# The second layer's scores, routing and experts in one phase, with the first tile routed in four parts

## The chip, the cores and the metric

One NeuronCore of a Trainium2 chip runs the whole program. The metric is the device time of one execution in microseconds. The engines are TensorE (PE), VectorE (DVE), ScalarE (ACT), GpSimd (POOL) and SyncE (SP), each with an instruction queue of its own; they meet only at semaphores. SP starts plain transfers, GpSimd starts the gathers.

## The reference

Two blocks of two layers each, for 256 tokens of width 1024. The part at hand is the feed-forward sublayer of the first block, run for its second layer (`l = 1`), where only x is updated:

```python
def peer_ffn(h, w_query, sub_keys, u_tab, v_tab):          # chunks of 128 tokens
    q = (hc @ w_query).reshape(128, 8, 2, 64)
    s = einsum('chpd,hpnd->chpn', q, sub_keys)              # 8 heads, 2 lists of 128 scores
    s_top, i_top = top_k(s, 16)
    cand = s_top[:, :, 0, :, None] + s_top[:, :, 1, None, :]   # 16 x 16 sums a head
    best, pos = top_k(cand, 16)
    eid = take_along_axis(i_top0 * 128 + i_top1, pos)       # 16 experts a head, 128 a token
    gate = softmax(best)
    act = gelu(einsum('chkd,cd->chk', u_tab[eid], hc)) * gate
    return einsum('chk,chkd->cd', act, v_tab[eid])
```

Each token needs 128 rows of `u_tab` and 128 rows of `v_tab`, each of 4 KB.

## The kernel before, in words

The program is a row of phases. `phase` opens a block with one program per engine and ends with a barrier of all engines. A function given as `ahead` is run by SP in a phase to load what the next phase reads first. `done` makes an engine wait for its own instruction's semaphore. Buffers are SBUF tiles; `ps` is PSUM, 8 banks of 512 columns.

For the second layer three phases follow each other:

1. `norm_modulate` computes h from x; ahead it loads the first half of `w_query` into `wring` slot 0 (`first_unit`).
2. `scores` (lines 1317 to 1402). SP loads the keys, the numbers 0 to 15 (`iot`) and the second half of `w_query`. For each of 8 heads TensorE computes the query (L1361), ScalarE copies it (L1387), TensorE multiplies it with the keys (L1352), and ScalarE copies the scores of tile 0 (128 tokens) to `sc` (L1374) and those of tile 1 to `stage` (L1379), from where SP stores them to DRAM (`kept`). VectorE follows head by head: `route_list` ranks each of a head's two lists (`best16`, L1242 to L1246), `route_sums` makes the 256 sums (L1257, L1259), `route_head` ranks them. After the eighth head `route_tail` runs for all heads at once: `route_shift` (L1268), `route_pick` (L1276 to L1286, six instructions over 128 x 16 = 2048 columns, which turn positions into list entries), `route_ids` (L1290, L1291, the expert numbers `eid`), `route_gate` (L1297 to L1299) after ScalarE's Exp (L1314).
3. `experts` (from line 1943). The work is 2 tiles x 16 groups `G` of `GRP = 8` expert columns; a head is two groups. For each group GpSimd issues 8 gathers of u rows into `gu` (L2036) and 8 of v rows into `gv` (L2045), 512 KB each. There is one buffer per column: a gather of `gu` waits for the dot product of the group before on the same buffer, a gather of `gv` for the accumulation (`summed`, columns 0 to 3) or the matmul (`mixed`, columns 4 to 7) of the group before. VectorE runs, in this order for each group, `dot` (8 dot products with the token rows `htok`, L2116), `route_next`, `weigh` (L2123, after ScalarE's Gelu, L2065) and `add_up` (4 accumulations, L2134 and L2136). ScalarE makes diagonal matrices (L2074) and TensorE adds the other four columns with them (L2010). At the start TensorE turns h (`turn_h`, L1984) and ScalarE copies it to `htok` (`copy_h`, L2053).

`route_next` routes tile 1 beside the groups of tile 0, out of `sc`, which SP has loaded back from DRAM (L2084): 3 lists in each of the first groups until 16 are done, the sums at G = 5, one head in each of G = 6 to 13, and the tail at G = 14. Beside tile 1 the phase builds rows of a bias table for the next block.

The order of work on each engine is the order in which the code is written. GpSimd enters the `experts` phase only after the barrier that ends `scores`.

Of the kernel before, what the change touches and what calls it, by code (L numbers as in the profile page):

```python
# [97 lines left out]
class Program:  # L98
# [1134 lines left out]
    def memory_scores(self):  # L1233
        self.sc = self.sb("sc", [P, 16, NKEY])
        self.qp = self.sb("qp", [P, 2, 2 * S])
        self.keys = self.sb("keys", [P, H1, 2 * NKEY])
        self.stage = self.sb("stage", [P, 2, 3, 2 * NKEY])

# [9 lines left out]
    def route_list(self, dve, sig, g):  # L1248

        self.best16(dve, sig, self.sc[:, g, :], self.sc[:, g, :], self.top[:, g, :], self.topi[:, g, :])  # L1250
# [15 lines left out]
    def route_shift(self, dve, shifted, t):  # L1266
        g3 = self.gate[:, t, :].rearrange("p (h k) -> p h k", h=H1)
        done(dve, self.nc.vector.tensor_tensor(g3, self.best[:], self.best[:, :, 0:1].to_broadcast([P, H1, TOPK]), ALU.subtract),  # L1268
             shifted)

    def route_pick(self, dve, sig, part):

        v = self.nc.vector
        bpos, bhi, bhf, hot = self.bpos, self.bhi, self.bhf, self.hot
        if part == 0:
            done(dve, v.tensor_scalar(bhi[:, 0, :], bpos[:], 4, None, ALU.logical_shift_right), sig)  # L1276
            done(dve, v.tensor_scalar(bhi[:, 1, :], bpos[:], 15, None, ALU.bitwise_and), sig)
            done(dve, v.tensor_copy(bhf[:], bhi[:]), sig)
            return
        c = part - 1  # L1280
        tf = self.topf[:].rearrange("p (h c) k -> p h c k", c=2)
        done(dve, v.tensor_tensor(hot, bhf[:, c, :].unsqueeze(2).to_broadcast([P, COLS, TOPK]),
                                  self.iot[:].unsqueeze(1).to_broadcast([P, COLS, TOPK]), ALU.is_equal), sig)
        hh = hot.rearrange("p (h k) i -> p h k i", h=H1)
        done(dve, v.tensor_tensor(hh, hh, tf[:, :, c, :].unsqueeze(2).to_broadcast([P, H1, TOPK, TOPK]), ALU.mult), sig)
        done(dve, v.tensor_reduce(self.esel[:, c, :], hot, AX, ALU.add), sig)  # L1286

    def route_ids(self, dve, sig, l, t):
        v, esel = self.nc.vector, self.esel
        done(dve, v.scalar_tensor_tensor(esel[:, 0, :], esel[:, 0, :], float(NKEY), esel[:, 1, :], ALU.mult, ALU.add), sig)  # L1290
        done(dve, v.tensor_scalar(self.eid[:, t, :], esel[:, 0, :], float(l * NEXP), None, ALU.add), sig)  # L1291

    def route_gate(self, dve, sig, exped, t, nth):
        v, gsum = self.nc.vector, self.gsum
        g3 = self.gate[:, t, :].rearrange("p (h k) -> p h k", h=H1)
        dve.wait_ge(exped.sem, nth)
        done(dve, v.tensor_reduce(gsum[:], g3, AX, ALU.add), sig)  # L1297
        done(dve, v.reciprocal(gsum[:], gsum[:]), sig)
        done(dve, v.tensor_tensor(g3, g3, gsum[:].unsqueeze(2).to_broadcast([P, H1, TOPK]), ALU.mult), sig)  # L1299

    def route_tail(self, dve, sig, shifted, exped, l, t, nth=1):
        self.route_shift(dve, shifted, t)
        for part in range(3):
            self.route_pick(dve, sig, part)
        self.route_ids(dve, sig, l, t)
        self.route_gate(dve, sig, exped, t, nth)

    def route_exp(self, act, shifted, exped, t):
        act.wait_ge(shifted.sem, 1)
        self.route_exp_now(act, exped, t)  # L1310

    def route_exp_now(self, act, exped, t):
        g = self.gate[:, t, :]
        self.nc.scalar.activation(g, g, ACT.Exp).then_inc(exped.sem, 1)  # L1314

    def scores(self, l, T, weights):


        nc, ps, a, hT = self.nc, self.ps, self.a, self.hT
        tiles = T // P  # L1320
        qp, keys, sc, stage = self.qp, self.keys, self.sc, self.stage

        def slot(s):
            return self.wring[:, s, 0:KD * 512].rearrange("p (k n) -> p k n", k=KD)

        def bank(h, t):
            return ps[:, 4 + 2 * (h % 2) + t // 2, (t % 2) * 256:(t % 2) * 256 + 256]
        with self.phase("loaded", "w1", "full", "copied", "sfull", "first", "rest", "shifted", "dve_done", "exped",
                        "stored0", "stored1") as (
                block, loaded, w1, full, copied, sfull, first, rest, shifted, dd, exped, st0, st1):  # L1330
            st = (st0, st1)

            @block.sync
            def _(sp):
                sp.dma_start(keys[:], a["keys"][l]).then_inc(loaded.sem, 16)
                sp.dma_start(self.iot[:], a["iota16"]).then_inc(loaded.sem, 16)
                sp.dma_start(slot(1), weights(1)).then_inc(w1.sem, 16)
                for h in range(H1):
                    sp.wait_ge(rest.sem, h + 1)
                    sp.dma_start(self.kept[1:tiles, :, h * 256:(h + 1) * 256].rearrange("t p n -> p t n"),  # L1340
                                 stage[:, h % 2, 0:tiles - 1, :]).then_inc(st[h % 2].sem, 16)
                for s in range(2):
                    sp.wait_ge(st[s].sem, 16 * H1 // 2)

            @block.tensor
            def _(pe):
                def score(h):
                    pe.wait_ge(copied.sem, h + 1)
                    if h >= 2:
                        pe.wait_ge(rest.sem, h - 1)  # L1350
                    for t in range(tiles):
                        m = nc.tensor.matmul(bank(h, t), qp[:, h % 2, t * P:(t + 1) * P], keys[:, h, :], start=True, stop=True)  # L1352
                    m.then_inc(sfull.sem, 1)

                for h in range(H1):
                    if h == 4:
                        pe.wait_ge(w1.sem, 16)
                    if h >= 4:
                        pe.wait_ge(copied.sem, h - 3)
                    for k in range(KD):  # L1360
                        m = nc.tensor.matmul(ps[:, h % 4, 0:T], slot(h // 4)[:, k, (h % 4) * P:(h % 4 + 1) * P],  # L1361
                                             hT[:, k, 0:T], start=k == 0, stop=k == KD - 1)
                    m.then_inc(full.sem, 1)
                    if h == 0:
                        pe.wait_ge(loaded.sem, 32)
                    else:
                        score(h - 1)
                score(H1 - 1)

            @block.scalar  # L1370
            def _(act):
                def out(h):
                    act.wait_ge(sfull.sem, h + 1)
                    nc.scalar.activation(sc[:, 2 * h:2 * h + 2, :].rearrange("p a n -> p (a n)"), bank(h, 0),  # L1374
                                         ACT.Copy).then_inc(first.sem, 1)
                    if h >= 2:
                        act.wait_ge(st[h % 2].sem, 16 * (h // 2))
                    for t in range(1, tiles):
                        ins = nc.scalar.activation(stage[:, h % 2, t - 1, :], bank(h, t), ACT.Copy)  # L1379
                        if t == tiles - 1:  # L1380
                            ins.then_inc(rest.sem, 1)

                for h in range(H1):
                    act.wait_ge(full.sem, h + 1)
                    if h >= 2:
                        act.wait_ge(sfull.sem, h - 1)
                    nc.scalar.activation(qp[:, h % 2, 0:T], ps[:, h % 4, 0:T], ACT.Copy).then_inc(copied.sem, 1)  # L1387
                    if h >= 1:
                        out(h - 1)
                out(H1 - 1)  # L1390
                self.route_exp(act, shifted, exped, 0)

            @block.vector
            def _(dve):
                dve.wait_ge(loaded.sem, 32)
                for h in range(H1):
                    dve.wait_ge(first.sem, h + 1)
                    for g in (2 * h, 2 * h + 1):
                        self.route_list(dve, dd, g)
                    self.route_sums(dve, dd, slice(h, h + 1))  # L1400
                    self.route_head(dve, dd, h)
                self.route_tail(dve, dd, shifted, exped, l, 0)
# [538 lines left out]
    def experts(self, l, tiles, tables):  # L1941
# [25 lines left out]
        with self.phase("turned", "hready", "dotted", "gelud", "weighed", "summed", "diagd", "mixed", "joined", "turned2",  # L1967
# [114 lines left out]
            def _(sp):  # L2082
# [19 lines left out]
                if tables:  # L2102
                    for k in range(4):
                        sp.wait_ge(stored[k].sem, 64)
# [739 lines left out]
```

## Time and profile before

| | us |
|---|---|
| median of 3 runs (lowest, highest) | 4629.44 (4618.14, 4631.32) |
| the profiled execution, its own time | 4630.75 |
| its span in the trace | 4629.0 |
| PE, DVE, POOL, ACT busy in the span | 3687.6, 2507.9, 1346.4, 632.5 |
| scores phase, first matmul to last VectorE instruction | 2366.85 to 2449.04 |
| first gather; last instruction of `experts` | 2450.70; 3169.3 |

A row of a timeline gives start, duration, engine, line, operation, output and inputs, count, and in brackets the idle time before it with what ended it. A row of the stage table gives the busy time of each engine in a stretch with its number of instructions, the granted TensorE clock as a share of full speed, the share of time in which the DMA engines were busy, and what they moved.

### The profile page before, as it was taken

The page shows a single profiled execution, that of the slowest core. Times are in us where ns is not written, and L with a number is a line of the kernel's source. Part 1 is how long each engine was busy: PE and PEld are TensorE (multiplying, and loading weights), DVE is VectorE, ACT ScalarE, POOL GpSimd, SP SyncE. Part 2 cuts the span into 40 slices and gives each one's busy share as a digit, 9 for nine tenths or more (in the row PEclk, how much of TensorE's full clock was granted, in tenths as well). Part 3 has the DMA queues.
Part 4 walks back from the last instruction along what each step waited for, and adds up shares of the span by engine and source line. Part 5 has one row for each costly group of instructions (what it writes and reads, how often), then busy time and mean ns, then how long its engine had stood idle before and what let it go on. Part 6 is the DMA issues. An engine that isn't in the chain of part 4 may idle for free. (4 is left out here: it accounts for less than half of the span.)

```text
span 4629.0 us, 46599 instructions
## 1 busy us (share of the span) xinstructions
PE 3687.6 (80%) x15786; PEld 2896.0 (63%) x15786; DVE 2507.9 (54%) x4821; ACT 632.5 (14%) x1702; POOL 1346.4 (29%) x1156
## 2 busy tenths in 40 slices
PE   5889897588998999957962444546999898999898
PEld 2467685577777877734851111214886787887787
DVE  2365476977788677744558888673534101433300
ACT  2231111310000000023110001101012201011200
POOL 0260000146566566604006777771000000000000
PEclk7879998899999999977986677777996899997799
DMA  4308454689999999910928999996850343861243
GB/s 140 128 31 242 132 162 163 203 308 409 409 408 374 409 409 407 403 62 26 255 77 309 375 384 377 411 403 248 297 175 28 123 150 130 275 215 46 91 154 100
DMA packets 564560, 1093.55 MB, mean 236 GB/s; under 512 B 29796, under 2 KB 344164, under 8 KB 563590
## 3 DMA queue, kind: packets, MB, share of 16 engines
q1 hardware_dynamic: 412776, 549.92, 35.2%
q0 software_dynamic: 147456, 536.94, 29.7%
q10 hardware_dynamic: 4128, 4.19, 0.3%
q8 instruction: 105, 1.72, 0.2%
q14 instruction: 95, 0.78, 0.1%
HBM read 1074.16 MB, written 16.78 MB: 236 GB/s over the span
## 5 line engine op out<-in xcount | busy, mean ns | idle before, releaser
L2010 PE MATMUL ps<-gv,diag 128*128 128x512 f32 x512 | 302.0, 756 | 392.7 <-DMA gv<-in_v_tab,eid 290.0
L1728 POOL DMA_INDIRECT gu<-in_u_tab,eid x256 | 351.4, 1373 | 859.1 <-DVE gate L1299 509.1
L2457 PE MATMUL ps<-hT,wring 128*128 128x256 f32 x2560 | 559.2, 379 | 0.2 <-DMA wring<-in_ffn_w_up 0.2
L1693 PE MATMUL ps<-hT,wring 128*128 128x256 f32 x2048 | 481.0, 389 | 75.9 <-DVE hT L1866 75.9
L2457 PEld LDWEIGHTS ps<-hT,wring 128*128 128x128 f32 x2560 | 486.3, 190 | 66.7 <-issue 0.6
L1693 PEld LDWEIGHTS ps<-hT,wring 128*128 128x128 f32 x2048 | 387.1, 193 | 163.9 <-DVE hT L1866 113.2
L2010 PEld LDWEIGHTS ps<-gv,diag 128*128 128x128 f32 x512 | 123.0, 248 | 570.0 <-issue 425.4
L1684 PE MATMUL ps<-hT,wring 128*128 128x256 f32 x2048 | 466.4, 381 | 6.8 <-DMA wring<-in_u_first 6.8
L1684 PEld LDWEIGHTS ps<-hT,wring 128*128 128x128 f32 x2048 | 391.6, 191 | 60.7 <-DMA wring<-in_u_first 6.9
L1890 DVE SCALAR_TENSOR_TENSOR wring<-gv,wgt,wring 128x1024 f32<-128x1024 f32 x254 | 326.5, 1286 | 115.6 <-DMA gv<-in_v_tab,eid 111.9
L2116 DVE CUSTOM_DVE_ANT_0 junk<-gu,htok 128x1024 f32<-128x1024 f32 x256 | 313.7, 1225 | 130.5 <-DMA gu<-in_u_tab,eid 121.8
L2036 POOL DMA_INDIRECT gu<-in_u_tab,eid x256 | 275.8, 1077 | 349.7 <-POOLq L134 272.0
L1873 DVE CUSTOM_DVE_ANT_0 gu<-gu,htok 128x1024 f32<-128x1024 f32 x256 | 313.2, 1223 | 116.9 <-DMA gu<-in_u_tab,eid 114.4
L1735 POOL DMA_INDIRECT gv<-in_v_tab,eid x256 | 293.0, 1145 | 141.0 <-issue 73.3
L2468 PE MATMUL ps<-hff,wring 128*128 128x256 f32 x1408 | 310.4, 379 | 0.0
L2524 DVE TENSOR_TENSOR hff<-sgf,ps 128x256 f32<-128x256 f32 x88 | 35.6, 419 | 502.2 <-ACT sgf L2497 502.2
L2045 POOL DMA_INDIRECT gv<-in_v_tab,eid x256 | 269.1, 1051 | 79.2 <-issue 76.2
L2468 PEld LDWEIGHTS ps<-hff,wring 128*128 128x128 f32 x1408 | 267.5, 190 | 36.4
L1000 PE MATMUL ps<-hT,wring 128*128 128x256 f32 x768 | 179.7, 388 | 13.5 <-SPq L134 8.0
L1000 PEld LDWEIGHTS ps<-hT,wring 128*128 128x128 f32 x768 | 148.1, 195 | 35.4 <-issue 15.0
L2136 DVE SCALAR_TENSOR_TENSOR acc<-gv,wgt,acc 128x1024 f32<-128x1024 f32 x126 | 162.0, 1285 | 10.1 <-DMA gv<-in_v_tab,eid 5.9
L2497 ACT ACTIVATE sgf<-ps 128x256 f32<-128x256 f32 x88 | 33.7, 383 | 818.7 <-PE ps L2457 771.0
(332 smaller groups left out, 4836.9 us busy)
## 6 DMA issues: line engine op xcount, KB each, us to landing
wring<-in_u_first SPq DMA_DIRECT2D x128, 512.0 KB, 9.0
wring<-in_v_tab SPq DMA_DIRECT2D x128, 512.0 KB, 6.8
lslot<-in_ada_w SPq DMA_DIRECT2D x32, 1536.0 KB, 10.9
wring<-in_ffn_w_gate SPq DMA_DIRECT2D x44, 1024.0 KB, 7.5
wring<-in_ffn_w_up SPq DMA_DIRECT2D x44, 1024.0 KB, 10.0
wring<-in_ffn_w_down SPq DMA_DIRECT2D x44, 1024.0 KB, 5.0
wring<-in_w_in SPq DMA_DIRECT2D x72, 512.0 KB, 6.7
wring<-in_w_mod SPq DMA_DIRECT2D x28, 1024.0 KB, 7.0
```

Of the source, the lines that this page charges most:

```text
L1000: nc.tensor.matmul(ps[:, b, 0:T], slot(s, b)[:, k, :], hT[:, k, at:at + T], start=k == 0, stop=k == KD - 1)
L1684: m = nc.tensor.matmul(ps[:, 4 + e % 2, 0:S], uslot[:, e % 3, k, :], hT[:, k, S:2 * S], start=k == 0, stop=k == KD - 1)
L1693: m = nc.tensor.matmul(ps[:, n // 2, (n % 2) * S:(n % 2 + 1) * S], vslot[:, e % 2, n * P:(n + 1) * P], act_[:, e % 3, :], start=e == 0 and ...
L1728: nc.gpsimd.indirect_dma_start(gu[:, n % RING, :], None, ub, bass.IndirectOffsetOnAxis(ap=eid[:, n // COLS, n % COLS:n % COLS + 1], axis=0 ...
L1735: nc.gpsimd.indirect_dma_start(gv[:, n % RING, :], None, vb, bass.IndirectOffsetOnAxis(ap=eid[:, n // COLS, n % COLS:n % COLS + 1], axis=0 ...
L1873: v.tensor_tensor_reduce(out=gu[:, j, :], in0=gu[:, j, :], in1=htok[:, n // COLS, :], scale=1.0, scalar=0.0, op0=ALU.mult, op1=ALU.add, ac ...
L1890: ins = v.scalar_tensor_tensor(acc, gv[:, j, :], wgt[:, s, j:j + 1], acc, ALU.mult, ALU.add)
L2010: m = nc.tensor.matmul(ps[:, mixed_banks(t) + b, :], diag[:, s, i, :], gv[:, BYDVE + i, b * 512:(b + 1) * 512], start=first, stop=last)
L2036: nc.gpsimd.indirect_dma_start(gu[:, j, :], None, ub, bass.IndirectOffsetOnAxis(ap=eid[:, t, n * GRP + j:n * GRP + j + 1], axis=0)).then_i ...
L2116: v.tensor_tensor_reduce(out=junk[:], in0=gu[:, j, :], in1=htok[:, t % 2, :], scale=1.0, scalar=0.0, op0=ALU.mult, op1=ALU.add, accum_out= ...
L2457: m = nc.tensor.matmul(ps[:, 4 + 2 * s + n, q * S:(q + 1) * S], up_slot(s, q)[:, k, n * P:(n + 1) * P], hT[:, k, 0:S], start=k == 0, stop= ...
L2468: m = nc.tensor.matmul(ps[:, n // 2, (n % 2) * S:(n % 2 + 1) * S], down_slot(s)[:, k, n * P:(n + 1) * P], hff[:, s, k, :], start=first and ...
```

## The change

The `scores` phase is gone and its work goes to the start of `experts`. The keys are loaded in the norm phase before, into the half of `xT` that held the context (`query_and_keys`). The scores of tile 1 are copied to the free half of `hT` (`later`) and never leave the chip. The first tile is routed in four parts (`PARTS`): head 0, head 1, heads 2 and 3, heads 4 to 7; the tail functions take a range of heads. GpSimd waits on `listed` only where a group needs the numbers of a new part (`PART_OF_GROUP`). VectorE ranks head 0, chooses its numbers, does the same with head 1, then starts the groups; the other heads of tile 0 are ranked in groups 0 to 5, their numbers chosen in groups 1 and 6, and tile 1 is routed in groups 7 to 14. The turn of h stands behind the query of the third head on TensorE, its copy behind that of the fourth on ScalarE.

```diff
+    def query_and_keys(self, l, weights):
+        def start(sp, landed):
+            sp.dma_start(self.wring[:, 0, 0:KD * 512].rearrange("p (k n) -> p k n", k=KD), weights(0)).then_inc(landed.sem, 16)
+            sp.dma_start(self.xT[:, :, S:2 * S], self.a["keys"][l]).then_inc(landed.sem, 16)
+            sp.dma_start(self.iot[:], self.a["iota16"]).then_inc(landed.sem, 16)
+            return 3
+        return start
...
-        LISTS, HEADS, TAIL = 3, 6, 14
+        PARTS = [(0, slice(0, 1)), (0, slice(1, 2)), (0, slice(2, 4)), (0, slice(4, 8)), (1, slice(0, 8))]
+        PART_OF_GROUP = {0: 1, 2: 2, 4: 3, 8: 4, 16: 5}
+        TAIL_AT = {2: 1, 3: 6, 4: 14}
+        LIST_FROM, HEADS_FROM = 7, 11
+        qp, keys, sc, later = self.qp, self.xT[:, :, S:2 * S], self.sc, self.hT[:, :, S:2 * S]
...
             def _(pe):
-                turn_h(0)
+                for h in range(H1):
...
+                    m.then_inc(full.sem, 1)
+                    if h:
+                        score(h - 1)
+                    if h == 2:
+                        turn_h(0)
+                score(H1 - 1)
...
             def _(pool):
-                    if n == 0 and t >= 1:
-                        pool.wait_ge(routed.sem, ROUTED * (t - 1) + EID)
+                    if G in PART_OF_GROUP:
+                        pool.wait_ge(listed.sem, PART_OF_GROUP[G])
...
             def _(act):
-                copy_h(0)
+                for h in range(H1):
...
+                    nc.scalar.activation(qp[:, h % 2, :], ps[:, h % 4, 0:S], ACT.Copy).then_inc(copied.sem, 1)
+                    if h >= 1:
+                        out(h - 1)
+                    if h == 3:
+                        copy_h(0)
+                out(H1 - 1)
+                exp_part(0)
+                exp_part(1)
...
             def _(dve):
+                def head_lists(h):
+                    dve.wait_ge(first.sem, h + 1)
+                    for g in (2 * h, 2 * h + 1):
+                        self.route_list(dve, routed, g)
+                    self.route_sums(dve, routed, slice(h, h + 1))
+                    self.route_head(dve, routed, h)
+
+                def pick_part(i):
+                    t, heads = PARTS[i]
+                    self.route_shift(dve, shifted, t, heads)
+                    for part in range(3):
+                        self.route_pick(dve, routed, part, heads)
+                    self.route_ids(dve, routed, l, t, heads, listed)
...
+                def route_ahead(G):
+                    if G < 2:
+                        head_lists(2 + G)
+                    elif G < 6:
+                        head_lists(2 + G)
+                    elif LIST_FROM <= G < LIST_FROM + 4:
...
+                        for g in range(4 * (G - LIST_FROM), 4 * (G - LIST_FROM) + 4):
+                            self.route_list(dve, routed, g, later[:, g // 2, g % 2 * NKEY:(g % 2 + 1) * NKEY])
+                    elif HEADS_FROM <= G < HEADS_FROM + 3:
+                        if G == HEADS_FROM:
+                            self.route_sums(dve, routed, slice(0, H1))
+                        for h in range(3 * (G - HEADS_FROM), min(3 * (G - HEADS_FROM) + 3, H1)):
+                            self.route_head(dve, routed, h)
+                    for i, at in TAIL_AT.items():
+                        if at == G:
+                            pick_part(i)
+                            gate_part(i)
+
+                for h in range(2):
+                    head_lists(h)
+                    pick_part(h)
                 for G in range(ALL):
...
-                    route_next(G)
+                    if G == 0:
+                        gate_part(0)
+                        gate_part(1)
+                    route_ahead(G)
                     weigh(G)
                     add_up(G)
...
-            self.norm_modulate(S, A_G2, 3, 4, ahead=self.first_unit(w_of("w_query")))
-            self.memory_scores()
-            self.scores(l, S, w_of("w_query"))
-            self.release(mixer)
+            self.norm_modulate(S, A_G2, 3, 4, ahead=self.query_and_keys(l, w_of("w_query")))
             self.memory_gather()
-            self.experts(l, 2, True)
+            self.experts(l, w_of("w_query"))
```

How the instructions stand now is shown at two places of VectorE's queue. The first is the end of routing of tile 0 and the first dot product. Before, behind the ranking of the eighth head (`ISA junk` is a dot product):

```order
L1246 MAX_INDEX bpos<-best,wring 128x8
L1268 TENSOR_TENSOR gate<-best 128x128
...
L1282 TENSOR_TENSOR wring<-bhf,iot 128x2048
L1285 TENSOR_TENSOR wring<-wring,topf 128x2048
L1286 TENSOR_REDUCE esel<-wring 128x128
...
L1291 TENSOR_SCALAR eid<-esel 128x128
L1297 TENSOR_REDUCE gsum<-gate 128x8
L1298 RECIPROCAL gsum<-gsum 128x8
L1299 TENSOR_TENSOR gate<-gate,gsum 128x128
L126 UNCONDITIONAL_BRANCH
L2106 UNCONDITIONAL_BRANCH
L2116 ISA junk,dots<-gu,htok 128x1024
```

Now, behind the ranking of head 1 (that of head 0 ends in the same rows):

```order
L1240 MAX_INDEX bpos<-best,wring 128x8
L1266 TENSOR_TENSOR gate<-best 128x16
...
L1281 TENSOR_TENSOR wring<-bhf,iot 128x256
L1284 TENSOR_TENSOR wring<-wring,topf 128x256
L1285 TENSOR_REDUCE esel<-wring 128x16
...
L1290 SCALAR_TENSOR_TENSOR esel<-esel 128x16
L1291 TENSOR_SCALAR eid<-esel 128x16
L2073 ISA junk,dots<-gu,htok 128x1024
```

The dot products begin behind two heads instead of eight, the wide instructions have 256 columns, and no end of a phase lies between. The second place is group 1, behind its dot products, where before three lists of tile 1 stood and then `L2123 TENSOR_TENSOR wgt<-wgt,gate 128x8`:

```order
L1253 TENSOR_TENSOR wring<-top 128x256
...
L1240 MAX_INDEX bpos<-best,wring 128x8
L1266 TENSOR_TENSOR gate<-best 128x32
...
L1284 TENSOR_TENSOR wring<-wring,topf 128x512
L1285 TENSOR_REDUCE esel<-wring 128x32
L1290 SCALAR_TENSOR_TENSOR esel<-esel 128x32
L1291 TENSOR_SCALAR eid<-esel 128x32
L1298 TENSOR_REDUCE gsum<-gate 128x2
L1299 RECIPROCAL gsum<-gsum 128x2
L1300 TENSOR_TENSOR gate<-gate,gsum 128x32
L2080 TENSOR_TENSOR wgt<-wgt,gate 128x8
L2093 SCALAR_TENSOR_TENSOR acc<-gv,wgt,acc 128x1024 x4
```

Head 3 of tile 0 and the numbers of heads 2 and 3 stand between the dot products of group 1 and its accumulations.

## Rows read from the trace of the kernel before

**Rows 1.** Stage table: scoring, gathers of tile 0 (columns: section above)

```profile
2372.00:2404.00 32.00, 31.74 (x148) 27.59 (x146) 24.22 (x102) 7.90 (x23) 0.00 (x0) 1.00 0.23 82
2451.00:2778.00 327.00, 133.27 (x237) 55.17 (x235) 270.04 (x505) 24.35 (x76) 254.74 (x238) 0.68 0.99 379
```

**Rows 2.** Timeline: routing of tile 0 on DVE, first gather, first dot product

```profile
2377.51 0.29 DVE L1242 MAX8 top<-sc 128x8 f32<-128x128 f32 x1 [12.26 <-ACT sc L1374]
...
2384.38 0.30 DVE L1242 MAX8 top<-sc 128x8 f32<-128x128 f32 x1
...
2432.48 0.29 DVE L1268 TENSOR_TENSOR gate<-best 128x128 f32<-128x128 f32 x1
...
2447.93 0.23 DVE L1291 TENSOR_SCALAR eid<-esel 128x128 uint32<-128x128 f32 x1
...
2450.70 1.02 POOL L2036 DMA_INDIRECT gu<-in_u_tab,eid  x1 [272.00 <-POOLq L134]
...
2456.67 1.23 DVE L2116 CUSTOM_DVE_ANT_0 junk<-gu,htok 128x1024 f32<-128x1024 f32 x1 [7.63 <-DMA gu<-in_u_tab,eid]
```

**Rows 3.** Timeline of DVE in the experts phase: groups 0, 13, 14 and 15

```profile
2473.48 0.17 DVE L2123 TENSOR_TENSOR wgt<-wgt,gate 128x8 f32<-128x8 f32 x1
...
2755.98 0.43 DVE L1242 MAX8 best<-wring 128x8 f32<-128x256 f32 x1
...
2758.49 0.17 DVE L2123 TENSOR_TENSOR wgt<-wgt,gate 128x8 f32<-128x8 f32 x1
...
2777.79 0.29 DVE L1268 TENSOR_TENSOR gate<-best 128x128 f32<-128x128 f32 x1
...
2794.46 0.17 DVE L2123 TENSOR_TENSOR wgt<-wgt,gate 128x8 f32<-128x8 f32 x1
...
2799.94 1.22 DVE L2116 CUSTOM_DVE_ANT_0 junk<-gu,htok 128x1024 f32<-128x1024 f32 x1
...
2815.87 1.22 DVE L2116 CUSTOM_DVE_ANT_0 junk<-gu,htok 128x1024 f32<-128x1024 f32 x1
```

**Rows 4.** Timeline of ACT: the Gelu of groups 0, 6, 18 and 31

```profile
2467.95 0.21 ACT L2065 ACTIVATE wgt<-dots 128x8 f32<-128x8 f32 x1 [13.54 <-DVE dots L2116]
...
2602.22 0.21 ACT L2065 ACTIVATE wgt<-dots 128x8 f32<-128x8 f32 x1 [16.82 <-DVE dots L2116]
...
2869.63 0.21 ACT L2065 ACTIVATE wgt<-dots 128x8 f32<-128x8 f32 x1 [5.78 <-DVE dots L2116]
...
3148.64 0.21 ACT L2065 ACTIVATE wgt<-dots 128x8 f32<-128x8 f32 x1 [18.63 <-DVE dots L2116]
```

**Rows 5.** Idle of DVE before tile 0's dot products (us, times); POOL at group 15

```profile
  DMA gu<-in_u_tab,eid: 48.4, 38
...
2796.75 1.32 POOL L2045 DMA_INDIRECT gv<-in_v_tab,eid  x1 [1.52 <-DVE acc L2136]
```

**Rows 6.** Entry: issue and landing of w_query, end of the norm, last score copy

```profile
2354.51 0.37 SPq L146 DMA_DIRECT2D wring<-in_w_query  x1
...
wring<-in_w_query SPq DMA_DIRECT2D x1, 2048.0 KB, 8.5
...
2362.07 4.04 ACT L342 ACTIVATE hT<-hT,mod,aff 128x256 f32<-128x256 f32 x8 [2.35 <-DVE hT L364]
...
2404.06 0.38 ACT L1379 ACTIVATE stage<-ps 128x256 f32<-128x256 f32 x1
```

**Rows 7.** Timeline: gathers beside wide DVE instructions and a dot product

```profile
2507.84 1.22 DVE L2116 CUSTOM_DVE_ANT_0 junk<-gu,htok 128x1024 f32<-128x1024 f32 x1
2508.91 0.97 POOL L2045 DMA_INDIRECT gv<-in_v_tab,eid  x1 [0.30 <-issue]
...
2781.29 2.29 DVE L1285 TENSOR_TENSOR wring<-wring,topf 128x2048 f32<-128x2048 f32 x1
2782.37 2.02 POOL L2036 DMA_INDIRECT gu<-in_u_tab,eid  x1 [0.30 <-issue]
2784.70 0.94 POOL L2036 DMA_INDIRECT gu<-in_u_tab,eid  x1 [0.31 <-issue]
```

More of the change, by code:

```diff
@@ L1264, in route_head, with gates_of @@
         self.best16(dve, sig, self.cand[:, h, :], self.cand[:, h, :], self.best[:, h, :], self.bpos[:, h * TOPK:(h + 1) * TOPK])
[L1266 to L1271, printed above, removed]
+    def gates_of(self, t, heads):
+        return self.gate[:, t, heads.start * TOPK:heads.stop * TOPK]
@@ L1279, in route_pick @@
             return
         c = part - 1
[L1281 to L1286, printed above, removed]
@@ L1301, in route_tail @@
[L1301 to L1313, printed above, removed]
-        self.nc.scalar.activation(g, g, ACT.Exp).then_inc(exped.sem, 1)
@@ L1316, in scores @@
[L1316 to L1402, printed above, removed]
@@ new lines, in route_ids, with route_gate @@
+    def route_ids(self, dve, sig, l, t, heads=slice(0, H1), ready=None):
+        v, at = self.nc.vector, slice(heads.start * TOPK, heads.stop * TOPK)
+        e0, e1 = self.esel[:, 0, at], self.esel[:, 1, at]
+        done(dve, v.scalar_tensor_tensor(e0, e0, float(NKEY), e1, ALU.mult, ALU.add), sig)
+        done(dve, v.tensor_scalar(self.eid[:, t, at], e0, float(l * NEXP), None, ALU.add), ready or sig)
+    def route_gate(self, dve, sig, exped, t, nth, heads=slice(0, H1)):
+        v, gsum = self.nc.vector, self.gsum[:, heads]
+        n = heads.stop - heads.start
+        g3 = self.gates_of(t, heads).rearrange("p (h k) -> p h k", h=n)
+        dve.wait_ge(exped.sem, nth)
+        done(dve, v.tensor_reduce(gsum, g3, AX, ALU.add), sig)
+        done(dve, v.reciprocal(gsum, gsum), sig)
+        done(dve, v.tensor_tensor(g3, g3, gsum.unsqueeze(2).to_broadcast([P, n, TOPK]), ALU.mult), sig)
@@ L1404, in memory_scores_first, with route_exp_now @@
+    def route_exp_now(self, act, exped, t, heads=slice(0, H1)):
+        g = self.gates_of(t, heads)
+        self.nc.scalar.activation(g, g, ACT.Exp).then_inc(exped.sem, 1)
     def memory_scores_first(self):
@@ L1998, in row, with score @@
                                      stop=True).then_inc(rowfull.sem, 1)
-                turn_h(0)
+                def score(h):
+                    pe.wait_ge(copied.sem, h + 1)
+                    if h >= 2:
+                        pe.wait_ge(rest.sem, h - 1)
+                    for t in range(2):
+                        m = nc.tensor.matmul(ps[:, 4 + h % 2, t * 256:(t + 1) * 256], qp[:, h % 2, t * P:(t + 1) * P], keys[:, h, :],
+                                             start=True, stop=True)
+                    m.then_inc(sfull.sem, 1)
+                for h in range(H1):
+                    if h == 4:
+                        pe.wait_ge(w1.sem, 16)
+                    if h >= 4:
+                        pe.wait_ge(copied.sem, h - 3)
+                    for k in range(KD):
+                        m = nc.tensor.matmul(ps[:, h % 4, 0:S], slot(h // 4)[:, k, (h % 4) * P:(h % 4 + 1) * P],
+                                             hT[:, k, 0:S], start=k == 0, stop=k == KD - 1)
+                    m.then_inc(full.sem, 1)
[4 more added lines that the diff above has]
+                score(H1 - 1)
                 for G in range(ALL):
```

108 lines of the change are left out of this document (53 added, 55 removed).

## Prediction

> **What bounds the kernel now.** I read the page first. Then the stage table, the timelines of VectorE, ScalarE and GpSimd around the change, and the waits. In the stage that the change touches the DMA engines are busy for 0.99 of the time and GpSimd issues one gather behind another, while TensorE has only 133 of 327 us to do [rows 1]. In the 32 us before that the order is the reverse: DMA share 0.23, TensorE at full clock, and VectorE routing the first tile [rows 1]. That is the stretch to look at. Its first head is picked from 2377.51 to 2384.38, that is 6.87 us a head (16 lists of 128, the pair sums, one list of 256), the eighth ends at 2432.48, the choice of the expert numbers for all heads lasts to 2448.16, and the first gather starts at 2450.70, the first dot product at 2456.67 [rows 2]. For 73 us almost nothing moves on the memory side, and afterwards the memory side is the bound.
>
> How much of a gather period VectorE needs decides what an early start is worth. A group of 8 expert columns is 16 gathers, 8 dot products and 4 accumulations. From the dot product at 2799.94 to that at 2815.87, with no wait for data, it is 15.93 us; where routing stands between, it hides ScalarE's Gelu (0.3 us), so I use **15.65 us a group** [rows 3]. Gelu starts give the period: 2467.95 to 2602.22 is 6 groups of 22.38 us, 2602.22 to 2777.79 is 8 of 21.95, and tile 1 runs at 21.46 (2869.63 to 3148.64, 13 groups) [rows 3, 4]. In the first six groups VectorE also ranks 3 lists of the next tile (5.53 us, 2467.95 to 2473.48), in the next eight one head (2.51 us, 2755.98 to 2758.49) [rows 3, 4]. So the load is 21.2, 18.2 and 15.65 us and VectorE waits 1.2, 3.8 and 5.8 us a group. In all it waits 48.4 us for the gathered u rows in tile 0, 7.6 of them before the first dot [rows 2, 5].
>
> **The change, part by part.**
>
> *Start of the gathers.* Scores come out as before. Head 0 is ranked at 2384.35, then its numbers are chosen alone: six wide instructions on 256 elements instead of 2048. A 256-wide one takes 0.43 and a 2048-wide one 2.29 us [rows 3, 7], a line of 0.16 + 0.00104 a column. Six at 0.46 with the gap and six narrow ones at 0.2 make 4.0 us, so the numbers are there at 2388.35 and the first gather follows some 0.3 us later, 62 us earlier than before. Head 1 costs 6.87 + 4.0 and VectorE reaches the first dot product at 2399.2; the first row landed 6.0 us after its issue before [rows 2], at 2394.7 now, so it does not wait. **The first dot product moves by -57.5 us.** The copy of the scores of tile 1 stays on the chip: 2 MB of stores and loads go, among them the 1 MB load beside the first gathers; I count nothing, since the stores lie under routing and the load under a wait of VectorE that now is gone.
>
> *What VectorE then does beside the gathers.* Before, the 15 groups from the first dot to that at 2799.94 held 15 x 15.65 - 0.5 (the first accumulation is a short one) = 234.2 us, 16 lists 29.5, pair sums 2.7, eight heads 20.1 and the tail 16.7 (2777.79 to 2794.46) [rows 3]: 303.2 us of work in 343.3 us, 40.1 us waited. Now the same 234.2 plus, by group: G0 the gates of heads 0 and 1 and head 2, 8.1; G1 head 3, the numbers for heads 2 and 3 (six at 0.72, narrow 1.2) and gates, 13.0; G2 to G5 one head each, 27.5; G6 the numbers for heads 4 to 7 (six at 1.25, narrow 1.4) and gates, 9.6; G7 to G10 four lists each, 29.5; G11 pair sums and three heads, 10.2; G12 7.5; G13 5.0; G14 the tail, 16.7. Sum 127.1, in all **361.3 us**. Nearly every group is now at 22.5 us or more, above the gathers' own pace, so VectorE is the bound of tile 0 and GpSimd waits.
>
> *Waits that stay.* They shrink with load: 5.8, 3.8, 1.2 us at 15.65, 18.2, 21.2. Bounds for a group at 22.5 to 23.2: nothing (after the 32 us tail group the next two run without a wait [rows 3]), and 1.2. I take 0.5, 1.2 for G13 alone and nearly nothing for G0, G1, G6, G11 and G14: 6 us in all, between 0 and 18.
>
> *Sum to the dot product of G15.* -57.5 + (361.3 + 6.0 - 343.3 = 24.0) = **-33.5 us**. At that point GpSimd stands as before: it is held at the gather of v behind the tail, since that buffer is freed by the accumulation (2796.75) [rows 5]. From there tile 1 is the same work, bound by the gathers, so the lead stays as it is.
>
> *Entry.* Keys and the 16 numbers now load during the norm, behind the query weights. The weights landed 8.5 us after 2354.51; the norm ends with ScalarE at 2366.11 [rows 6]. One more MB at the 379 GB/s of [rows 1] is 2.8 us: 2365.8, hidden by 0.3 us. The keys land in 1 KB pieces; twice the time would end at 2368.6, 2 us late. I take +0.5, bounds 0 and 2. Before, these loads were hidden, as TensorE waited for none of them.
>
> *Things at nothing.* The transpose of h (1.94 us TensorE) and its copy move between heads 2 and 3; TensorE and ScalarE are 27 us ahead of VectorE by the eighth head. The gate exponentials of heads 0 and 1 stand on ScalarE behind all eight score copies: these ended at 2404.44 before [rows 6], 2 us later now, plus the table and two short Exp, 2408.4; VectorE asks at 2409.4. GpSimd gets four new waits for numbers (G2, G4, G8, G16); behind them stand all later gathers, but the numbers are ready 22 us or more ahead each time. One phase boundary (2449.04 to 2450.0) is in the 62 us.
>
> *The lock between the two engines.* Issuing a gather took 2.02 us beside a 2048-wide VectorE instruction with two inputs and 0.94 beside the reduction that follows it, as wide but with one; beside a dot product of 1.22 us it took 0.97 [rows 7]. The instructions moved under gathers are 0.43, 0.69 and 1.22 us long, no longer than the dot product. So I add nothing.
> The Trainium skill (SBUF — State Buffer, section "SBUF: two separate sides") says that a VectorE instruction with two SBUF inputs and a GpSimd instruction reading SBUF exclude each other for the whole instruction. By that rule, the trace agrees. The page speaks against moving routing under gathers; that case is the second rival below, priced from rows.
>
> **Total**: 4630.75 (profiled execution; span 4629.0) - 33.5 + 0.5 = 4597.8; the median of the three runs shown is 1.3 us lower, so **4597 us** rounded. What the measurement can tell from no change is 0.3%, 14 us.
>
> **Rivals.**
> 1. *Waits come on top of the load* (ends on the other side). The chain gather, dot, free buffer, gather could leave each group a wait whatever VectorE does. For it: DMA share 0.99 [rows 1]. With 2.6 us a group the gain is gone, since the new load is 58 us larger and the head start 57.5; that is the point from which it decides. At 3.8 us, as in the eight head groups, it is 15 x 3.8 = 57 us of waits instead of 40: 4646. Against it: the falling series above. 5%, half of that within the 14 us.
> 2. *GpSimd is locked out.* If each moved two-input instruction held one gather for its length and GpSimd were then the later of the two: 4 x 0.69 + 4 x 1.22 + 6 x 0.43 = 10 us, 4607. Against it: in these groups GpSimd has slack. 8%.
> 3. *The parts do not follow at once*, the change does not do what it says. The gates of head 0 hang on the last score copy, with 1 us to spare. TensorE scored at a granted clock of 1.00, busy 31.74 of 32 us [rows 1]; if the clock fell to half there, the 27 us from the first score to the last would grow by up to 27 and VectorE would stand for up to 26 before its first accumulation; for half of that, 4610. Against it: the work before is unchanged. 4%.
> 4. *No waits at all, and the 1 MB load beside the first gathers was not free*: 6.0 + 2.8 us more gain, 4588. 8%.
> 5. The forecast, waits of 0 to 1.2 us: 4590 to 4609. 75%.
>
> **Range.** The forecast's own bounds, rivals 2, 3 and 4, and the 13 us spread of the three runs give 4582 to 4612. Faster by over 0.3% means below 4615.6: 0.92. Within: 0.05. Slower: 0.03.
>
> **What would show it.** The first gather near 2389 and first dot near 2399 (right if within 3 us); Gelu starts in tile 0 some 24.5 us apart on average, with 29 at G1; GpSimd idle for several us before v gathers in G2; VectorE's wait for u rows in tile 0 falling from 48 to under 15 us; the dot of G15 at 2766; tile 1 at 21.5 us a group. The forecast is wrong if VectorE still waits 2 us or more a group, if the norm phase grows by more than 2 us, or if tile 1 changes pace.

## Result, and the profile after

The changed kernel takes **4593.31 us** (median of 5 runs, 4580.05 to 4597.69) against 4627.66 for the kernel before in runs beside it; the ratio is 0.9921, 95% interval 0.9905 to 0.9936. It is 34 us faster, 33 were forecast, and 4593.3 lies in the range of 4582 to 4612. The profiled execution has a span of 4591.5 us, 37.5 less than before. Ratios and intervals here and below leave out one execution of the variant `all_ahead`, of 7698.77 us against some 4663 us for its nine others.

The stage table of the changed kernel, then the same stretches of the kernel before. The stretches are the scoring of [rows 1], first MAX8 to the first dot product of group 15, and from there to the Gelu of group 31:

```profile
2372.00:2404.00 32.00, 32.00 (x154) 28.23 (x153) 24.59 (x83) 8.32 (x24) 11.64 (x11) 1.00 0.46 167
...
2377.31:2760.32 383.01, 163.92 (x368) 80.25 (x368) 364.73 (x793) 42.79 (x113) 250.93 (x251) 0.70 0.91 341
2760.32:3111.98 351.66, 170.33 (x307) 69.08 (x305) 257.32 (x363) 33.34 (x96) 273.02 (x259) 0.72 1.01 396
```

```profile
2377.51:2799.94 422.43, 165.28 (x368) 81.09 (x367) 357.65 (x747) 37.18 (x106) 271.81 (x251) 0.68 0.82 313
2799.94:3148.64 348.70, 171.81 (x307) 69.46 (x305) 257.39 (x363) 33.34 (x96) 269.75 (x260) 0.73 1.02 401
```

VectorE has 7 us more to do (364.73 against 357.65, for the tail instructions are issued four times for tile 0), and yet its stretch is 39.4 us shorter. Outside its instructions it spends 18.3 us instead of 64.8. Those 18.3 us are the gaps between some 790 instructions, 0.02 us each on average, so from its first MAX8 to group 15 it never stands. The memory side is busy for 0.91 of the stretch instead of 0.82.

The timelines of VectorE and GpSimd (the last row is group 15) answer to [rows 2, 3]:

```profile
2384.18 0.17 DVE L1266 TENSOR_TENSOR gate<-best 128x16 f32<-128x16 f32 x1
...
2387.99 0.17 DVE L1291 TENSOR_SCALAR eid<-esel 128x16 uint32<-128x16 f32 x1
...
2399.12 1.23 DVE L2073 CUSTOM_DVE_ANT_0 junk<-gu,htok 128x1024 f32<-128x1024 f32 x1
...
2440.92 0.69 DVE L1284 TENSOR_TENSOR wring<-wring,topf 128x512 f32<-128x512 f32 x1
...
2760.32 1.23 DVE L2073 CUSTOM_DVE_ANT_0 junk<-gu,htok 128x1024 f32<-128x1024 f32 x1
```

```profile
2389.00 1.02 POOL L1980 DMA_INDIRECT gu<-in_u_tab,eid  x1 [210.58 <-DVE eid L1291]
...
2439.72 0.93 POOL L1980 DMA_INDIRECT gu<-in_u_tab,eid  x1 [0.31 <-issue]
2447.92 1.33 POOL L1989 DMA_INDIRECT gv<-in_v_tab,eid  x1 [7.27 <-DVE acc L2093]
```

The choice of head 0's numbers ends at 2388.16, 0.84 us later the first gather is issued, 61.7 us earlier than before. The row of the first dot product has no bracket: it does not wait. In groups 2 to 13, and again in group 15, GpSimd stands at the first v gather until VectorE's accumulation frees the buffer.

The timeline of ScalarE: the last score copy, the exponentials, and the Gelu of groups 0, 14, 15, 18, 19, 20 and 31, for [rows 4, 6]:

```profile
2404.82 0.38 ACT L2009 ACTIVATE hT<-ps 128x256 f32<-128x256 f32 x1
2405.21 1.28 ACT L1304 ACT_TABLE_LOAD   x1
2406.51 0.32 ACT L1304 ACTIVATE gate<-gate 128x16 f32<-128x16 f32 x2
...
2409.26 0.21 ACT L2030 ACTIVATE wgt<-dots 128x8 f32<-128x8 f32 x1 [1.13 <-DVE dots L2073]
...
2738.21 0.21 ACT L2030 ACTIVATE wgt<-dots 128x8 f32<-128x8 f32 x1 [14.14 <-DVE dots L2073]
2770.45 0.21 ACT L2030 ACTIVATE wgt<-dots 128x8 f32<-128x8 f32 x1 [12.84 <-DVE dots L2073]
...
2831.62 0.21 ACT L2030 ACTIVATE wgt<-dots 128x8 f32<-128x8 f32 x1 [5.62 <-DVE dots L2073]
2854.80 0.21 ACT L2030 ACTIVATE wgt<-dots 128x8 f32<-128x8 f32 x1 [4.89 <-DVE dots L2073]
2876.35 0.21 ACT L2030 ACTIVATE wgt<-dots 128x8 f32<-128x8 f32 x1 [3.27 <-DVE dots L2073]
...
3111.98 0.21 ACT L2030 ACTIVATE wgt<-dots 128x8 f32<-128x8 f32 x1 [19.00 <-DVE dots L2073]
```

Two sums of waits: GpSimd over both tiles, and VectorE in tile 1.

```profile
POOL gv L1989 <- DVE acc L2093: 47.5, 13, 9.8
...
DVE junk L2073 <- DMA gu<-in_u_tab,eid: 76.2, 27, 6.4
```

In tile 0 the roles are exchanged: VectorE waited 48.4 us for u rows [rows 5] and now not at all, while GpSimd waits 47.5 us for VectorE. In tile 1 VectorE waits 76.2 us for u rows; it was 73.4 before. There GpSimd's work is without a break: no wait of it is over 0.3 us, and its 273.02 us for 259 gathers with 0.30 us between them fill the stretch of 351.66. The DMA share is 1.01 in the same stretch. Which of the two limits sets the pace of tile 1 was not tested; below it is called the gathers' pace.

### The profile page after: what moved, and what is told of

Its sections match the earlier page's. It is cut to its first block and busy times, and to the rows that moved or that the text cites. A ratio compares the mean times of both kernels' runs of the same rounds, so it can differ in the third digit from the quotient of the medians.

```text
span 4591.5 us, 46621 instructions
## 1 busy us (share of the span) xinstructions
PE 3687.9 (80%) x15786; PEld 2896.5 (63%) x15786; DVE 2506.8 (55%) x4866; ACT 638.0 (14%) x1709; POOL 1331.4 (29%) x1156
## 5 line engine op out<-in xcount | busy, mean ns | idle before, releaser
L1630 POOL DMA_INDIRECT gu<-in_u_tab,eid x256 | 346.1, 1352 | 853.6 <-DVE gate L1300 508.0
L2073 DVE CUSTOM_DVE_ANT_0 junk<-gu,htok 128x1024 f32<-128x1024 f32 x256 | 313.6, 1225 | 85.6 <-DMA gu<-in_u_tab,eid 76.2
L1980 POOL DMA_INDIRECT gu<-in_u_tab,eid x256 | 263.4, 1029 | 289.0 <-DVE eid L1291 210.6
```

Source lines behind the costliest of these rows:

```text
L1630: nc.gpsimd.indirect_dma_start(gu[:, n % RING, :], None, ub, bass.IndirectOffsetOnAxis(ap=eid[:, n // COLS, n % COLS:n % COLS + 1], axis=0 ...
L2073: v.tensor_tensor_reduce(out=junk[:], in0=gu[:, j, :], in1=htok[:, t % 2, :], scale=1.0, scalar=0.0, op0=ALU.mult, op1=ALU.add, accum_out= ...
```

## Experiments

Twelve runs in three sets. The first set ran on one chip (A), the second on a second (B), the third on a third (C); each kernel's ratio is to the kernel before in the same set. Before took 4662.75 us on A, 4655.3 on B and 4628.32 on C, so times are compared within a set alone.

**Set 1 (A): how far ahead must routing be, and is VectorE the bound?** `four_ahead` routes heads 0 to 3 before the first gather, in three parts instead of five; heads 4 to 7 follow in groups 0 to 3, and the later groups' routing and the exponentials are moved to suit:

```diff
-        PARTS = [(0, slice(0, 1)), (0, slice(1, 2)), (0, slice(2, 4)), (0, slice(4, 8)), (1, slice(0, 8))]
-        PART_OF_GROUP = {0: 1, 2: 2, 4: 3, 8: 4, 16: 5}
+        PARTS = [(0, slice(0, 4)), (0, slice(4, 8)), (1, slice(0, 8))]
+        PART_OF_GROUP = {0: 1, 8: 2, 16: 3}
...
-                for h in range(2):
+                for h in range(4):
                     head_lists(h)
-                    pick_part(h)
+                pick_part(0)
```

> Edit: heads 0 to 3 are ranked and chosen together before the first group, heads 4 to 7 beside groups 0 to 4; the lists of tile 1 are spread over groups 5 to 10. Theory A (in tile 0 VectorE is the bound and never waits, so only its total work counts, and when the gathers start does not): work from 2377.3 is 27.5 + 8.8 ahead of the first dot product and 340 beside the groups, so the dot product of group 15 comes at about 2754, 6 us before the changed kernel's 2760.3, although the first gather starts 25 us later (2414 against 2389); time about 4587. Theory B (the earlier start of the gathers is what the change gains, each us of it): 25 us later means about 4618.

`all_ahead` routes the whole first tile before any gather. What is left of the change is the merged phase, the scores that stay on the chip and the keys loaded early.

```diff
+        PARTS = [(0, slice(0, 8)), (1, slice(0, 8))]
+        PART_OF_GROUP = {0: 1, 16: 2}
...
+                for h in range(H1):
                     head_lists(h)
+                pick_part(0)
```

> Edit: still one phase, but tile 0 is routed as a whole before the first gather and tile 1 as in the kernel before (three lists a group, then a head a group, tail at group 14). It isolates the merging of the phases and the scores that stay on the chip. Theory A: the gathers are the bound of tile 0 again, VectorE waits some 40 us in it as before, only the phase boundary goes: first gather near 2448, time about 4625 to 4628, within 0.1% of the kernel before. Theory B (the round trip of the scores through memory had cost something in the gathers, up to the 2.8 us of its 1 MB, and the boundary more than 2.5 us): up to 8 us faster than before, 4620.

`bydve3` and `bydve2` move one and two of the four accumulations a group from VectorE to TensorE, by one constant:

```diff
-BYDVE = 4
+BYDVE = 3
```

> Edit on the changed kernel: VectorE accumulates 3 of a group's 8 columns instead of 4, TensorE 5 instead of 4. Theory A: VectorE's load falls by 1.31 us in each of 15 groups, 19.7 us; loads of 21.2 us are at the gathers' own pace, so a part comes back as waits: dot product of group 15 at 2745 to 2752, time 4578 to 4585. Theory B (tile 0 is bound by the gathers, not by VectorE): no gain, and TensorE, which now needs about 12.5 us a group, ends the phase some 1 us later: 4593 to 4595.

> Edit on the changed kernel: VectorE accumulates 2 columns, TensorE 6. Theory A: VectorE's load falls by 39 us over tile 0, below the gathers' pace of 21.5 us in most groups; the gathers become the bound, the dot product of group 15 comes near 2399 + 15 x 21.9 = 2728 at best, time 4562 to 4575, if TensorE's 15 us a group do not hold the buffers of v (gathers of v wait for its matmuls; then less, up to nothing gained against the variant with 3). Theory B (gathers are the bound already): no gain, 4593 to 4597.

Measured: four_ahead 4639.52 us, ratio 0.995 (0.9936 to 0.9964); all_ahead 4663.47, 1.0003 (0.9988 to 1.0019); bydve3 4630.19, 0.9931 (0.991 to 0.9951); bydve2 4628.34, 0.9933 (0.9908 to 0.9957). The plain result is all_ahead: **merging the phases and keeping the scores on the chip is worth nothing that can be measured** (the interval runs from 6 us faster to 9 slower). four_ahead differs from it in the order of routing alone and is 24 us faster, with intervals that don't touch: **the gain comes from gathers that start before routing is done.** The other two couldn't be placed, as the changed kernel itself had not run on this chip. Taken as ratios to 4627.66, theory A put bydve3 at 0.989 to 0.991 and bydve2 at 0.986 to 0.989, theory B both near 0.993, and both came out where theory B had them. bydve2 has 19 us less VectorE work than bydve3 (326.45 against 345.73 us from the first MAX8 to group 15); its stretch is only 6.7 us shorter (396.40 against 403.14), and its time 1.9 us, inside the intervals.

**Set 2 (B): the changed kernel beside them, and added work.** `after_again`, `four_ahead_again` and `bydve3_again` repeat; `more_lists` ranks two more lists of 128 in each of groups 2 to 5, from scratch data into tiles of their own that nothing reads, so the output is unchanged:

```diff
                         head_lists(2 + G)
+                        for _ in range(2):
+                            self.best16(dve, routed, junk[:, 0:NKEY], junk[:, NKEY:2 * NKEY], self.xv[:], self.xi[:])
```

> The changed kernel as it is, beside the variants on one chip (the chip of the first set of variants ran the kernel before 35 us slower, with VectorE waiting 1 us behind single instructions of its own at times). Every theory expects the ratio on record, 0.992.

> The variant with four heads ranked ahead of the first group again, now beside the changed kernel. Theory A (VectorE's total work in tile 0 decides): 6 us under the changed kernel, ratio to the kernel before 0.991. Theory B (the start of the gathers decides): 20 us or more above the changed kernel, 0.996 or more. The first set gave 0.995 without the changed kernel beside it.

> VectorE accumulates 3 columns instead of 4, again, beside the changed kernel. Theory A: 8 to 15 us under the changed kernel. Theory B: within 2 us of it.

> Edit on the changed kernel: VectorE ranks two more lists (scratch data, results unused) in each of groups 2 to 5, 8 x 1.84 = 14.8 us more work; nothing else changes. Theory A (VectorE never waits in tile 0): all of it lands on the time, group periods 2 to 5 go from 22.5 to 26.2 us, dot product of group 15 14.8 us later, time +14.8 us. Theory B (the gathers are the bound): less than 5 us.

Measured: after_again 4628.79 us, ratio 0.994 (0.9927 to 0.9953); four_ahead_again 4633.33, 0.9951 (0.9938 to 0.9964); bydve3_again 4624.04, 0.9932 (0.9918 to 0.9947); more_lists 4640.92, 0.9971 (0.9958 to 0.9984). More_lists is 12.1 us slower than after_again: added VectorE work in these groups arrives in the total almost in full. The stretch from the first MAX8 to group 15 grows by 15.4 us (after_again first, then more_lists), for 13.4 us more VectorE work:

```profile
2372.64:2781.35 408.71, 161.89 (x368) 79.50 (x368) 364.70 (x793) 42.67 (x113) 252.66 (x251) 0.70 0.86 319
2369.51:2793.61 424.10, 168.57 (x368) 81.31 (x368) 378.07 (x856) 42.78 (x113) 252.51 (x251) 0.67 0.83 308
```

Its Gelu starts (the rows are groups 2 to 5) are 26.5 to 26.9 us apart, against 22.5 to 23.7 in after_again:

```profile
2471.81 0.21 ACT L2032 ACTIVATE wgt<-dots 128x8 f32<-128x8 f32 x1 [12.84 <-DVE dots L2075]
2498.26 0.21 ACT L2032 ACTIVATE wgt<-dots 128x8 f32<-128x8 f32 x1 [14.13 <-issue]
2524.79 0.21 ACT L2032 ACTIVATE wgt<-dots 128x8 f32<-128x8 f32 x1 [14.14 <-issue]
2551.65 0.21 ACT L2032 ACTIVATE wgt<-dots 128x8 f32<-128x8 f32 x1 [14.14 <-DVE dots L2075]
```

But bydve3_again, 19 us lighter, gained 4.8, and four_ahead_again lost 4.5, where neither theory had put it; both intervals overlap that of after_again. The profiles say more than the times. The stretch of bydve3_again is 394.91 us, 13.8 shorter than that of after_again. But in its execution the first MAX8 came 7.7 us later from the start of the kernel (2380.30 against 2372.64), in a part that no edit touches, and tile 1 took 3.7 us more (373.85 to the last Gelu). The stretch of four_ahead_again is 412.62 us, 3.9 longer. The waits of after_again from 2380 to 2430, and its ScalarE rows there, show something that the first profile did not have:

```profile
ACT qp L2019 <- remote: 20.4, 2, 14.2
PEld ps L1927 <- issue: 16.8, 1, 16.8
DVE gsum L1298 <- ACT gate L1304: 16.7, 1, 16.7
```

```profile
2397.23 0.38 ACT L2019 ACTIVATE qp<-ps 128x256 f32<-128x256 f32 x1 [6.20 <-remote]
...
2414.90 0.38 ACT L2019 ACTIVATE qp<-ps 128x256 f32<-128x256 f32 x1 [14.18 <-remote]
...
2420.93 0.32 ACT L1304 ACTIVATE gate<-gate 128x16 f32<-128x16 f32 x2
```

ScalarE stands twice between two copies, 6.20 and 14.18 us. TensorE's matmuls for these copies end at 2393.79 and 2398.10, that is 3.4 and 16.8 us before the copies start. The rest of the scores come late, the exponentials too, and VectorE stands 16.7 us at the gates of head 0. That is the place of rival 3, with a price of 16.7 us and another cause than the clock: TensorE had done its part. All five profiles on A and B with gathers that start behind head 0 have it: two stops of ScalarE, 20.4 to 24.1 us together, and 16.7 to 18.2 us at the gates. The three of four_ahead and all_ahead on the same chips, whose scores are done before the first gather, have neither. That is what the eight profiles show: on these chips the stops come where gathers run beside the score copies. That the gathers cause them is not shown, for no run held the gathers back on a chip that has the stops. It fits that four_ahead lost only 4.5 us: it starts its first dot product 20.1 us later from the first MAX8 (41.9 against 21.8 us), and does not pay the 16.7. From first MAX8 to group 15, VectorE's time outside its instructions on B was 44.0 us in after_again (408.71 less 364.70): 18.3 of gaps, 16.7 here, and 9 in short stops of at most 1.2 us.

**Set 3 (C): the stop, and the best version.** `v_held` holds GpSimd at the first v gather until the last score copy is done, so that only eight gathers run beside the scores:

```diff
+                    if G == 0:
+                        pool.wait_ge(rest.sem, H1)
+                        pool.sem_inc(slots.sem, 1)
```

> The changed kernel once more, as the base for the three kernels beside it. Ratio to the kernel before 0.991 to 0.995. On the chip of the second set ScalarE stopped twice in its score copies (6.2 and 14.2 us) while the first gathers ran, TensorE behind it, and VectorE stood 16.7 us at the gates of head 0; on the chip of the first profile nothing of this was seen. Whether it is here is read from this trace.

> GpSimd issues the eight u gathers of group 0 as in the changed kernel, but waits for the last score copy of ScalarE before the first v gather. Theory S (ScalarE stops because the gathers fill the DMA engines): where the changed kernel beside it has VectorE wait over 10 us at the gates of head 0, this one shows less than 6, the last score copy comes within 34 us of the first MAX8 (46 in the stalled profile, 27.5 in the free one), and the time is 3 to 12 us under the changed kernel. Theory T (the stop has another cause, such as ScalarE's own work): the wait stays over 10 us, and the time is the same or up to 5 us longer. Where the changed kernel beside it has no such wait, the accumulation of group 0 starts at about 33 us from the first MAX8 in both, and the times agree within 4 us.

> Three of eight accumulations a group on VectorE, five on TensorE. It was 4.8 us under the changed kernel on the same chip in the second set, and 9 above to 5 below by the first two. VectorE has 19 us less work in tile 0; the load bound lets up to 15 us of it through if the wait at the gates of head 0 is not there, 3 to 6 us if it is. Ratio to before 0.991 to 0.994.

> Both edits. If theory S holds, the two gains add up, since the one takes a wait away and the other takes work out of the groups: 8 to 15 us under the changed kernel beside it, ratio to before 0.989 to 0.992. If theory T holds or the stop isn't there: as with three accumulations alone, within 4 us.

Measured: after_third 4591.5 us, ratio 0.9924 (0.9907 to 0.9941); v_held 4596.27, 0.993 (0.9913 to 0.9947); bydve3_third **4572.71, 0.9877 (0.986 to 0.9894)**; v_held_bydve3 4577.58, 0.9886 (0.987 to 0.9902). On C no kernel shows the stop; from the first MAX8 to group 15 after_third takes 383.06 us, the first profile 383.01. So v_held could not test theory S against T; it shows that GpSimd can stand there for 7 us at little cost. The row is its first v gather:

```profile
2404.38 1.51 POOL L1992 DMA_INDIRECT gv<-in_v_tab,eid  x1 [6.96 <-ACT hT L2012]
```

Group 15 comes 1.75 us later from the first MAX8 than in after_third, and VectorE waits 1.8 us for u rows on the way; the times differ by 4.8, with overlapping intervals.

Without the stop the lighter VectorE pays in full. The stage table of after_third and of bydve3_third, first MAX8 to group 15, and GpSimd's wait for the accumulation in the latter:

```profile
2369.14:2752.20 383.06, 166.17 (x369) 80.66 (x369) 364.78 (x792) 42.79 (x113) 251.13 (x251) 0.70 0.91 341
```

```profile
2378.77:2742.27 363.50, 186.00 (x422) 90.01 (x422) 345.76 (x778) 47.16 (x128) 259.20 (x250) 0.74 0.94 358
...
POOL gv L1989 <- DVE acc L2093: 13.3, 4, 6.1
```

VectorE's work falls by 19.0 us, the stretch by 19.6, the kernel's time by 18.8. That the last agrees so well is in part luck: the stretch begins at 2369.14 in one profiled execution and at 2378.77 in the other, before anything that the edit touches, and these two executions differ by 11.1 us. **VectorE is the bound of tile 0**, shown from both sides by the stretch itself: more work by more_lists, less by bydve3_third. GpSimd's waits for the accumulation fall from 47.5 to 13.3 us, so about that much is left before the gathers' own pace. In tile 1 one accumulation less brings nothing (355.7 us from group 15 to the last Gelu against 355.3): there the gathers are the bound. v_held_bydve3 had no stop to remove here; its stretch is 366.15 us, 2.65 longer than that of bydve3_third, and VectorE waits 2.6 us for u rows in it. The difference of the two times, 4.9 us, is inside the intervals. `four_ahead` and `bydve2` were not run on C, so what they are worth where ScalarE doesn't stop is open: theory A, by which four_ahead would be 6 us faster than the changed kernel, is untested there. bydve3_third beats both kernels: 55.6 us under before, 18.8 under the changed kernel, with intervals that don't touch.

## Why the prediction was right, point by point

- *Start of the gathers.* Forecast: first gather 2388.7, first dot product 2399.2 without a wait. Measured 2389.00 and 2399.12, no wait. The dot moved by -57.55 us for a forecast of -57.5.
- *Work beside the groups.* Forecast 361.3 us from the first dot product to that of group 15. Measured 361.20 us, with no wait in it. Group by group it fits too: the heavy group 1 took 28.80 us for 28.65, group 14 32.24 for 32.35. A 512-wide instruction took 0.69 us; 0.72 was forecast with its gap. (A head ranks two lists of 128, not 16 as the prediction has it in one place; its 6.87 us are those of two.)
- *Waits that stay.* This is the mis-sized term: 6 us forecast, 0 measured, the low end of the 0 to 18. The series 5.8, 3.8, 1.2 was read as a property of one group's load. But a wait depends on GpSimd's lead, and the one group now below 22 us (group 13, Gelu to Gelu 20.6) lies between heavy ones; that the lead carried over it is what the missing wait says. This was the first half of rival 4.
- *Sum to group 15.* Forecast -33.5, measured -39.6 (2760.32 against 2799.94). **Of this 3.0 us are given back in tile 1**, where nothing was forecast: the lead by Gelu starts is 39.6 at group 15, 38.0 at group 18, 36.6 at group 19 and 36.7 at group 31 (2854.80 against 2891.38 and 3111.98 against 3148.64). Behind group 15 the load falls to 16 us, and VectorE catches up with the gathers in both kernels, so that alone takes nothing back. Of the 3.0 us, 1.6 are lost while GpSimd issues the u gathers of group 17: they take 13.48 us (2788.96 to 2802.44), before 11.86 (2828.58 to 2840.44), since more of them fell beside dot products (see rival 2). The rest, 1.4 us, comes between the Gelus of groups 18 and 19 and is not explained. No more than chance may be behind both: the changed kernel itself took 351.66 us from group 15 to the last Gelu in the first profile and 355.27 in after_third. The error of +6 and this one of -3 partly cancel, so the total fits better than its terms; that is luck.
- *Entry.* Forecast +0.5, bounds 0 and 2. From the issue of the query weights to the first matmul it is 12.52 us against 12.34: +0.2.
- *Scores stay on the chip, merged phase, priced at nothing.* all_ahead: ratio 1.0003 (0.9988 to 1.0019), so nothing above 9 us either way is hidden there. The 2.8 us of rival 4 can't be told from it.
- *Rival 1* (waits on top of the load) fell: the wait for u rows in tile 0 is 0. The time given for it, 4646, is 1 us low: by its own terms it is 4647. *Rival 2* (GpSimd locked out) is there in its mechanism, and it had no price here, since GpSimd had 47.5 us to spare in tile 0. The prediction read the 0.97 us of [rows 7] as free passage beside a dot product, but that gather starts 0.15 us before the dot product ends and so says little. In the profile after, 25 gathers start over 0.2 us before the end of a dot product, and each of them lasts that remainder and 0.80 to 0.82 us more. The first pair of rows is a wide reduction with one input, the second a dot product with two:

```profile
2744.04 2.29 DVE L1285 TENSOR_REDUCE esel<-wring 128x128 f32<-128x2048 f32 x1
2745.12 0.93 POOL L1980 DMA_INDIRECT gu<-in_u_tab,eid  x1 [0.30 <-issue]
...
2800.11 1.22 DVE L2073 CUSTOM_DVE_ANT_0 junk<-gu,htok 128x1024 f32<-128x1024 f32 x1 [1.06 <-DMA gu<-in_u_tab,eid]
2800.16 1.98 POOL L1980 DMA_INDIRECT gu<-in_u_tab,eid  x1 [0.30 <-issue]
```

So adding nothing was right because of GpSimd's slack, not because the moved instructions are short. Where GpSimd has no slack the same effect may cost something: in tile 1 its 259 gathers take 273.02 us, and at 0.94 each they would take 243.5 (an estimate from these rows).

- *Rival 3* (head 0's gates hang on the last score copy) did not occur in the profile that was forecast: the exponentials were done at 2406.83, VectorE asked at 2409.26. On chips A and B it occurred in every profile of that order of work. Its chance of 4% was set by the clock alone, which was 1.00 over the scoring; the slack of 2.4 us was the weak place, whatever uses it up.
- *The signs given.* Gelu starts in tile 0 24.1 us apart (24.5 forecast), 28.8 for 29 at the heavy group; GpSimd 7.27 us idle before the v gathers of group 2; tile 1 at 21.57 us a group for 21.5.

## What to carry to other kernels

When an engine that prepares work and one that fetches it take turns, start the fetches with the smallest part that can be prepared alone, and then sum the work of the preparing engine over the whole stretch: once it no longer waits, this sum is the time, and it held here to 0.1 us. Such an overlap makes the preparing engine the bound, so look next for work that another engine can take; here one constant gave another 18.8 us on chip C (on B the 4.8 us are within the noise). A wait that has 2 us of slack in one profile should be bounded by more than one profile, or moved: two of three other chips used it up several times over.

## What the runs showed of the hardware

- Three chips gave the same kernel before 4628.32, 4655.3 and 4662.75 us. The gain of the change was 0.994 (0.9927 to 0.9953) on B and 0.9924 (0.9907 to 0.9941) on C, with intervals that overlap; on A the changed kernel was not run.
- On B ScalarE stopped for 6.2 and 14.2 us in after_again, and for 20.4 to 24.1 us together in each of the five profiles on A and B with gathers beside the score copies. The records name no releaser on the core ("remote"). The transfers of the instruction queue were looked at as a cause: in after_again one ran at 2382 and the next at 2424, none in the stretch of 2391 to 2415 in which ScalarE stood. What stops it is open.
- In the profile after, a gather that GpSimd starts over 0.2 us before the end of a dot product, of the pair sums (L1253) or of a two-input TENSOR_TENSOR of the picks lasts until that instruction ends and 0.80 to 0.82 us more: up to 1.98 us beside a dot product of 1.22, 2.02 beside a 2048-wide instruction of 2.29. The one exception started at the same moment as a wide instruction, at 2746.36, and took 0.94. Beside MAX8 and the wide reduction a gather lasts 0.93 to 0.94 us, as it does beside nothing.
- On B, VectorE's added waits were many and short, mostly behind its own previous instruction; tile 1 of the same kernel took 370.2 us in after_again against 351.7 in the first profile (2781.35 to 3151.54), at a DMA share of 0.99 and 377 GB/s:

```profile
2781.35:3151.54 370.19, 171.12 (x307) 69.28 (x305) 257.33 (x363) 32.79 (x96) 275.50 (x259) 0.71 0.99 377
```
